# Scores of a product-key router by products with premultiplied weights: 512-column products on TensorE in place of 128-column queries and scores

## The reference, cut to what matters

```python
def peer(h, w_pq, sub_keys, u_tab, v_tab):
    B, N, D = h.shape                    # D = 1024
    T = B * N
    hf = h.reshape(T, D)
    q = (hf @ w_pq).reshape(T, PEER_HEADS, 2, PEER_HALF)          # 8 heads, 2 halves of 128
    s = jnp.einsum('thsd,hskd->thsk', q, sub_keys)                # 128 sub-keys per half
    s_top, i_top = lax.top_k(s, PEER_TOPK)                        # 16
    ...
```

## Time and profile before

| | us |
|---|---|
| median of 3 runs | 3248.2 (3245.08 to 3252.93) |
| profiled execution, its own time | 3257.12 |
| span of that profile | 3255.3 |
| PE busy | 3180.3 (98%) |
| DVE busy | 2619.6 (80%) |
| ACT busy | 1255.9 (39%) |
| POOL busy | 1592.9 (49%) |
| L1087 `query`, PE busy | 262.1 |

### The profile page before, as it was taken

One profiled execution on the slowest core, in us unless ns is written; L12 is line 12 of the kernel. 1 busy time (PEld: TensorE's weight loads), 2 busy tenths in 40 slices (PEclk: granted clock), 3 DMA queues, 4 the chain that ended last, 5 costly groups with the idle time before them and its releaser, 6 DMA issues.

```text
span 3255.3 us, 46922 instructions
## 1 busy us (share of the span) xinstructions
PE 3180.3 (98%) x17282; PEld 2784.5 (86%) x17282; DVE 2619.6 (80%) x5356; ACT 1255.9 (39%) x2309; POOL 1592.9 (49%) x999
## 2 busy tenths in 40 slices
PE   8999899999998899999999999999999999999998
PEld 5887588788877799898989999989999999999997
DVE  3333368888888799998989888889999998888876
ACT  3343334334426633333333333333433333333343
POOL 0300006788767388888888887323333332333310
PEclk9999999999999999999999999999999999999999
DMA  6924556676676799999999999989899999999963
GB/s 252 391 109 158 235 195 195 183 206 173 191 217 208 280 351 351 342 345 346 349 337 356 357 347 384 363 341 364 339 374 361 354 366 357 355 362 355 348 227 114
DMA packets 297746, 963.29 MB, mean 296 GB/s; under 512 B 94004, under 2 KB 148148, under 8 KB 238775
## 3 DMA queue, kind: packets, MB, share of 16 engines
q1 hardware_dynamic: 158680, 523.71, 43.9%
q0 software_dynamic: 138560, 436.55, 38.6%
q10 hardware_dynamic: 288, 0.16, 0.0%
HBM read 893.83 MB, written 66.49 MB: 295 GB/s over the span
## 4 chain that ended last, share of the span: by engine, by line
PE 47%; DVE 12%; DMA 5%; issue 1%; ACT 1%; SPq 0%; DVEq 0%; ACTq 0%
PE bank L1961 24%; PE bank L1971 23%; DMA work<-in_u 5%; DVE ring L2109 3%; DVE acc L2126 2%; DVE uL L2292 2%; DVE vL L2288 1%; DVE ga L2305 1%; DVE cL L2283 1%; ACT uR L2040 0%; ACT vR L2056 0%; DVE slots L2231 0%; DVE st L2258 0%; DVE work L2169 0%; DVE slots L2255 0%
## 5 line engine op out<-in xcount | busy, mean ns | idle before, releaser
L1923 POOL DMA_INDIRECT ring<-in_uv,slots x384 | 583.1, 1519 | 807.2 <-DVE carry L2126 698.1
L185 POOL DMA_INDIRECT g_cells<-slots x384 | 710.5, 1850 | 318.0 <-DVE slots L1639 199.7
L1961 PE MATMUL bank<-hR,uR 128*128 128x384 f32 x2032 | 684.9, 337 | 11.1 <-DVE uL L2292 11.0
L1961 PE MATMUL bank<-hR,uL 128*128 128x384 f32 x2032 | 684.3, 337 | 0.0
L1961 PE MATMUL bank<-hL,uR 128*128 128x384 f32 x2032 | 682.8, 336 | 0.0
L2048 ACT ACTIVATE cR<-ga 128x384 fp32r<-128x384 f32 x253 | 133.1, 526 | 945.2 <-PE bank L1971 569.1
L1971 PE MATMUL bank<-vR,cR 128*128 128x512 f32 x1518 | 472.8, 392 | 5.1 <-DVE cL L2283 4.5
L1971 PE MATMUL bank<-vR,cL 128*128 128x512 f32 x1518 | 471.1, 392 | 0.0
L1971 PE MATMUL bank<-vL,cR 128*128 128x512 f32 x1518 | 471.0, 391 | 0.0
L2109 DVE CUSTOM_DVE_ANT_0 ring<-ring,slots 128x1024 f32<-128x1024 f32 x384 | 467.2, 1254 | 1.9 <-DMA ring<-in_uv,slots 1.9
L1961 PEld LDWEIGHTS bank<-hR,uR 128*128 128x128 f32 x2032 | 383.2, 189 | 25.2 <-DVE uL L2292 15.6
(11 more groups left out here) (346 smaller groups left out, 4328.4 us busy)
## 6 DMA issues: line engine op xcount, KB each, us to landing
work<-in_v SPq DMA_DIRECT2D x256, 512.0 KB, 6.9
work<-in_u SPq DMA_DIRECT2D x254, 512.0 KB, 6.1
work<-in_w_pq SPq DMA_DIRECT2D x36, 2048.0 KB
work<-in_w_o SPq DMA_DIRECT2D x18, 2048.0 KB
g_cells<-work POOLq DMA_DIRECT2D x48, 512.0 KB, 5.6
work<-g_cells SPq DMA_DIRECT2D x32, 768.0 KB, 9.3
work<-g_blocks SPq DMA_DIRECT2D x31, 768.0 KB, 13.9
g_blocks<-big SPq DMA_DIRECT2D x8, 2048.0 KB, 6.8
```

The costliest lines, as they stand in the source:

```text
L185: pool.indirect_dma_start(out=cells_of(g_dram, i), out_offset=bass.IndirectOffsetOnAxis(ap=slots[:, i, D + k:D + k + 1].bitcast(U32), axis=0),
L1923: pool.indirect_dma_start(out=ring[:, k % R, :], out_offset=None, in_=a["uv"], in_offset=bass.IndirectOffsetOnAxis(ap=ids[:, k // P, k % P ...
L1961: mm = pe.matmul(A[t][:, 0:CW], w[t][:, k, :], h[:, k, :], start=(k == 0 and w is uR and h is hR), stop=(k == DK - 1 and w is uL))
```

## The change

In steps 3 to 6 PE multiplies the sub-keys into the query weights (`merge`): per step 8 banks of 4 products of 128 columns. ACT copies each bank into one of four buffers `merged` (it waits until the store four before has landed), and POOL stores each with a DMA of 256 KiB into a table `pq_scratch` in DRAM, 32 in all. From step 7 on, `score(i, g)` makes the scores at once by 8 products of 512 columns with the tile's rows held still and the stored table moving; `query`, its eviction and the buffer `qs` are gone. `sub` is loaded at the block's beginning instead of at step 4, and SP's order of 2 MiB loads has four new ones in it. DVE's two semaphores in `highest` become steps of its one chain semaphore, with the same waits.

```diff
+    MERGE = {3: 0, 4: 1, 5: 2, 6: 3}
...
+                    if key[0] == "score" and key[1] == 0:
+                        for m_out in merged_out:
+                            sp.wait_ge(m_out, FILLED + 2 * (key[2] + 1) * 16)
+                    part = key[1] if key[0] == "merge" else key[-1]
+                    src = {"mod": a["w_mod2"], "mix": a["w_o"], "merge": a["w_pqT"], "score": pq_dram}[key[0]]
+                    sp.dma_start(wr[:, at % 2, :], src[part, :, :]).then_inc(wr_in[at % 2], 16)
...
                         sp.wait_ge(w_mm, W["mod", 2] + 1)
+                        sp.dma_start(sub[:, :, :], a["sub"]).then_inc(const_in, 16)
                         load_x(0)
                         load_x(1)
+                        load("merge", 0, DK - 1)
...
+                    if n in MERGE and MERGE[n]:
+                        load("merge", MERGE[n], DK - 1)
                     if h == 1 and 0 <= i - 2 < NT:
-                        load("query", i - 2, 2)
+                        load("score", i - 2, 2)
...
+                for x in range(4 * DK):
+                    g, k = divmod(x, DK)
+                    pool.wait_ge(*emptied("merge", g, k))
+                    pool.dma_start(pq_dram[g, :, k * 512:(k + 1) * 512], merged[:, x % 4, :]).then_inc(merged_out[x % 4], 16)
...
-                def query(i, g):
+                def merge(g):
+                    if g == 0:
+                        pe.wait_ge(const_in, 16)
+                    w = weights("merge", g, DK - 1)
+                    for k in range(DK):
+                        ps = bank("merge", g, k)
+                        for l in range(4):
+                            mm = pe.matmul(ps[:, l * NKEY:(l + 1) * NKEY], w[:, l * D + k * P:l * D + (k + 1) * P],
+                                           sub[:, 4 * g + l, :], start=True, stop=True)
+                        mm.then_inc(w_mm, 1)
+
+                def score(i, g):
                     if g == 0:
                         pe.wait_ge(*emptied("turn", i, 0))
                         pe.wait_ge(*emptied("turn", i, 1))
-                    w, ps = weights("query", i, g), bank("query", i, g)
-                    for l in range(4):
-                        for k in range(DK):
-                            at = (l * DK + k) * P
-                            mm = pe.matmul(ps[:, l * P:(l + 1) * P], w[:, at:at + P], slots[:, i, k * P:(k + 1) * P],
-                                           start=(k == 0), stop=(k == DK - 1))
-                    mm.then_inc(w_mm, 1)
-
-                def score(i, g):
-                    ps = bank("score", i, g)
-                    pe.wait_ge(*emptied("query", i, g))
-                    if i == 0 and g == 0:
-                        pe.wait_ge(const_in, 48)
-                    for l in range(4):
-                        mm = pe.matmul(ps[:, l * NKEY:(l + 1) * NKEY], qs[:, g % 2, l, :], sub[:, 4 * g + l, :],
-                                       start=True, stop=True)
+                    w, ps = weights("score", i, g), bank("score", i, g)
+                    for k in range(DK):
+                        mm = pe.matmul(ps[:, :], slots[:, i, k * P:(k + 1) * P], w[:, k * 512:(k + 1) * 512],
+                                       start=(k == 0), stop=(k == DK - 1))
                     mm.then_inc(w_mm, 1)
...
-                def query(i, g):
-                    ps, f = bank("query", i, g)
-                    n = 4 * i + g
-                    if n >= 2:
-                        p = ("score", (n - 2) // 4, (n - 2) % 4)
-                        act.wait_ge(w_mm, W[p] + 1)
-                    act.activation(qs[:, g % 2, :, :], ps[:, :].rearrange("p (l t) -> p l t", l=4),
-                                   ACT.Copy).then_inc(f, 1)
+                def merge(g):
+                    for k in range(DK):
+                        ps, f = bank("merge", g, k)
+                        x = DK * g + k
+                        if x >= 4:
+                            act.wait_ge(merged_out[x % 4], FILLED + x // 4 * 16)
+                        act.activation(merged[:, x % 4, :], ps[:, :], ACT.Copy).then_inc(f, 1)
```

More of the change, by code:

```diff
@@ L64 @@
 EARLY = 16
+FILLED = (NZ // 4 + P // TB) * 16
 RATE = (2, 4)
@@ L248, in mixer_inputs @@
         junk = sq
-        zeroed = [sem(f"a_zero{k}") for k in range(4)]
+        pool_out = [sem(f"a_poolout{k}") for k in range(4)]
         zero_set, bias_in, pad_ready = sem("a_zset"), sem("a_bias"), sem("a_pad")
@@ L710, in _, with middle @@
                 finish(pe, NT - 1)
-def middle(nc, a, sb, sem, PS, ident, modc, sp1, silu, slots, carry, work, first_in, big, krT, kT, vv, front, mod_in, x1_dram, gate_dram, g_dram, placed, mix_dram, tile_in, tile_out, a_mm, a_ev, g_in, ga):
+    return pool_out
+def middle(nc, a, sb, sem, PS, ident, modc, sp1, silu, slots, carry, work, first_in, big, krT, kT, vv, front, mod_in, x1_dram, gate_dram, g_dram, placed, mix_dram, tile_in, tile_out, a_mm, a_ev, g_in, ga, pq_dram, merged_out):
     NH = NT * H
@@ L724, in number @@
         W[key] = len(W)
-        if key[0] in ("mix", "query") or key[0] == "mod" and key[1] in (3, 4):
+        if key[0] in ("mix", "score") or key[0] == "merge" and key[2] == DK - 1 or key[0] == "mod" and key[1] in (3, 4):
             WEIGHTS.append(key)
@@ L742, in middle @@
         if h == 1 and 0 <= i - 2 < NT:
-            number("query", i - 2, 2)
+            number("score", i - 2, 2)
         if h == 2:
-            if 0 <= i - 2 < NT and i - 1 != LAST:
-                number("score", i - 2, 2)
             if 0 <= i - 1 < NT:
@@ L762, in middle @@
             if 0 <= i - 1 < NT:
-                number("query", i - 1, 0)
-                number("query", i - 1, 1)
                 number("score", i - 1, 0)
+                number("score", i - 1, 1)
+        if n in MERGE:
+            for k in range(DK):
+                number("merge", MERGE[n], k)
     for ch_ in (6, 7):
@@ L1238, in _ @@
                         if 0 <= i - 1 < NT:
-                            query(i - 1, 0)
-                            query(i - 1, 1)
                             score(i - 1, 0)
+                            score(i - 1, 1)
+                    if n in MERGE:
+                        merge(MERGE[n])
                     if n == NH + 2:
@@ L1318, in spread @@
                         act.wait_ge(decoded, i)
+                    elif g == 0:
+                        for m_out in merged_out:
+                            act.wait_ge(m_out, FILLED + DK * 16)
                     sl = slice(4 * g, 4 * g + 4)
@@ L1418, in _ @@
                     if h == 2:
-                        if 0 <= i - 2 < NT and i - 1 != LAST:
-                            score(i - 2, 2)
                         if 0 <= i - 1 < NT:
@@ L1434, in _ @@
                             use(ch)
-                    if h == 0 and 0 <= i - 2 < NT:
-                        score(i - 2, 1)
                     if h == 0 and i - 1 == LAST:
@@ L1492, in highest @@
                         ins = dve.reduce_max(part[:, b:b + 1], PS[b][:, 0:width(n, b)], AX.X)
-                    ins.then_inc(m_part, 1)
-                    dve.wait_ge(m_part, n + 1)
-                    dve.reduce_max(mx[:, :], part[:, 0:groups(n)], AX.X).then_inc(m_max, 1)
-                    dve.wait_ge(m_max, n + 1)
+                    ch.step(ins)
+                    ch.step(dve.reduce_max(mx[:, :], part[:, 0:groups(n)], AX.X))
                     if n >= 2:
```

75 lines of the change are left out of this document (28 added, 47 removed).

## The result

The changed kernel takes 3265.94 us (median of 5 runs, 3263.57 to 3268.46), the kernel before 3249.65 in the same session (5 runs, 3245.08 to 3254.37). The ratio is 1.0044, 95% interval 1.0033 to 1.0055: slower by 0.44%. The forecast was 3246.2 with a range up to 3259, so the time lies outside it, on the slow side. A ratio is estimated from all the runs and can differ by about 0.1% from the quotient of two medians. The medians of the kernel before, run beside each group of experiments, lie from 3249.65 to 3252.43.

What follows compares the result with a forecast made beforehand. Attention block taken as bound by PE and an equally long DVE chain through norm; the merge's 29.3 us less savings of 31.3 gives -2.0 us, 3248.2 to 3246.2 us, with an 8-in-10 range of 3234 to 3259.

Steps and rivals of the forecast that it cites:

- the merge costs 29.3 us: Steps 3 to 6: the four merges, with their new waits, make step 7 begin 29.3 us later.
- the upper bound of 36: Steps 3 to 6: the most the four merges were to cost, 36 us; the lower bound was 24.4.
- 1 for stores: Step 3: 1 us added to the merge for its stores to DRAM.
- 1.5 for stores: Step 4: 1.5 us added to the merge for its stores to DRAM.
- The second weights: Step 4: the next merge weights, issued once mix's first half is used, take about 7 us for 2 MiB.
- The landing of the first weights: Step 3: the first merge's weights, with sub now ahead of them, land at 352.8.
- The tie of DVE's chain: Steps 12 to 31: DVE's run holds norm, so 2.7 us a tile arrive, 13.7 in all; 9.3 are given back.
- the rival that PE is the only bound: Steps 12 to 31: DVE's chain doesn't hold, the 9.3 us arrive too, 3232 to 3237; chance 0.17.
- The last attention head ends in step 35 and with it this tie: From step 32 to DVE's third one_hot unit: eight groups save 9.3 us; 11.5 us taken for the stretch.
- the 7.5 of the text: Block's tail: the part of the saving that falls behind the last mix, some 7.5 us.
- POOL was not hidden: Block's end: POOL's scatters end at 1073, the load needing the last at 1077, so just hidden.
- the merge's transfers stall PE: Steps 3 to 5: ACT waits for stores, PE for weights; at 5 us more per merge 3266; chance 0.15.

Runs made afterwards that it cites:

- holding the loads back: Changed kernel, four buffers; SP holds two 2 MiB loads (first half of mix, merge(2)) until a merge's first four stores have landed: 3261.86 us, ratio 1.0031.
- decode first: Changed kernel with DVE's decode ahead of the maxima at h = 0 (tiles 3 to 8), ACT's spread ahead of turned: 3247.94 us, ratio 0.9997.
- The twin kernel: Kernel before with only the 8 MiB DRAM table declared and never used: 3250.73 us, ratio 1.0001.
- the shortened DVE operation: Changed kernel with one operation of residual_in cut from 1024 to 8 columns: 3254.46 us, ratio 1.0015.
- both repairs: Changed kernel with eight merged buffers in place of four, and DVE's decode ahead of the maxima at h = 0: 3242.47 us, ratio 0.9971.

## Why the prediction was wrong, point by point

**The step that failed is the merge's price**, "so the merge costs 29.3 us": it cost 39.5, over the upper bound of 36 too. Two of its terms were mis-sized and one was missing.
- *Stores.* I gave "1 for stores" in step 3 and "1.5 for stores" in step 4, and had written in the bounds that in a full queue a store is "2 to 4 us late in each of steps 3 and 4". The lateness in the bounds came true: PE stood 2.99 and 4.06 us. I took the idle landing of the earlier trace rows as the value and left the loaded one for the range. Eight buffers, which remove just this, gave back 7.7 us, 5.9 of them beyond scatter; holding the loads back gave back 8.5.
- *The clock after a stand.* I counted a start at 1.2 GHz in step 3 only, as 2.7 us for which I showed no row. That size was about right: the eight banks of step 3 took 9.13 us without the stand, 2.0 over 7.15, and 9.13, 9.46 and 10.06 in the three kernels with eight buffers. For steps 4 and 5 I had put it at nothing. In step 5 the first attention products and the banks behind the stand ran partly at the low clock: six banks took 7.15 us instead of 5.36, the attention 7.35 instead of 6.1. Together 3.0 us, where step 5 was over by 2.9. In step 4 the two banks behind the stand took 3.58 us instead of 1.79, at a granted clock of 0.50. With eight buffers step 4 had no stand, and the attention of step 5 took 6.1 again (400.87 - 394.77), but the banks behind `high` 8.34.
- *The second weights* were reckoned to land 7 us after their issue; from 382.71 (369.74 + 6.1 + 6.87) to 391.16 it was 8.45. With 2.6 for the stand and 1.8 for the clock this makes 5.8 of the 6.2 us that step 4 was over.

The landing of the first weights (352.8 predicted, 357.62 less the 5.0 us of the late first block is 352.6) and step 6 (16.6, measured 16.62) held.

**The tie of DVE's chain held.** "Two chains of equal length lie side by side, and the change shortens one": 15.6 us arrived in the five tiles where PE alone would have given 23 (9.3 more than the 13.7 forecast), PE waited for `norm` at both places named, by 0.4 to 0.8 us, and shortening DVE by 1.06 us shortened the tile by 1.00. Only its size was off: 3.1 us a tile arrived instead of 2.7. With it the rival that PE is the only bound (3232 to 3237) is refuted in the changed kernel, and made true in the kernel with decode first, 67.17 us a tile against the 67.2 that I had given for it.

**"The last attention head ends in step 35 and with it this tie"** was half right. Step 32 still has its `decode`, and steps 32 to 35 took 70.35 us where decode first makes them 66.56. Of the 11.5 us forecast from step 32 on, 9.4 came: 2.0 up to step 36 and 7.4 behind it, against the 7.5 of the text.

**POOL was not hidden, though this cost nothing that shows.** The prediction had the scatters end at 1073, 4 us before the load that needs the last of them. They ended at 1115.67 - 21.19 = 1094.5, or 1089.5 without the 5.0 us of the late first block: 16.5 later than reckoned. Some 10 of these are the merge, the rest the scatters themselves, which took 482.1 us from 612.35 on where the kernel before took 475.5 from 577.27. The load then waited for them, as SP's waits of 1040 to 1160 us show:

```profile
SPq L958 <- DMA g_blocks<-slots: 6.5, 1, 6.5
```

The kernel before has no such wait. The load went out at 1098.66, 17.0 us before the block's end instead of 23.2. The experts lost nothing by it: they took 2.0 us less than before.

**From the trace to the median.** I let the changed kernel's profile stand 8.9 us over its runs, as that of before did. It stood 2.5 over. Of the 19.7 us between forecast and result, 10.3 are the block (10.2 of it the merge), 6.4 this assumption, and 3.0 the first block and the experts. The twin kernel points to what was behind most of the 6.4: with the same work its block was 5.6 us shorter than that of the profiled execution of before, by 3.2 in the very steps from 1 to 7 on which the merge's price was reckoned and by 2.3 behind step 36. Against the two undisturbed traces of the kernel before (63.8 and 63.9 us from step 1 to step 7) the merge costs 42.6, as much as the ratios give for leaving it out.

**The rival that came true, in part,** is "the merge's transfers stall PE". Each merge had to lose over 2.1 us more than I gave it, and on average they lost 2.6 (10.2 / 4): 1.1 up to step 4, 6.2 in step 4, 2.9 in step 5 and none in step 6. In step 5 no transfer was waited for, so the transfers and the clock behind their stands account for 7.3, or 1.8 a merge. That the time is close to the 3266 written there is chance, since 9.5 of its 19.7 us over the forecast are no part of the merge. I gave it 0.15, because the DMA share in steps 4 to 6 would be lower than at 340 to 360 us. It was (0.72, 0.74 and 0.54 over the three windows of 20 us from 360 to 420), and the mean hid the case that counts, a 2 MiB load issued just as the stores begin.

## What to carry to other kernels

- Where a buffer's turn fits with nothing to spare in an idle queue, take the landing beside the loads that the program issues at that moment, not the idle one. Here the difference was some 6 to 8 us, and four more buffers removed it.
- Before taking work from the engine that is busy for 100% of a stretch, look for the engine that hands it its next input, and shorten both chains: here a reorder on DVE, worth less than nothing before, was worth 12 us after the change.
- One trace of before is one execution. Where the sum rests on a stretch of 30 us, a second trace of the same code tells how much of it is scatter (3 us here; in the changed kernel's merges 4, from 102.3 to 106.6 us in the four kernels in which neither buffers nor loads differ).

## What was not expected of the hardware

The same stand was followed by a different clock from one kernel to the next. In step 5 PE stands 2.87 us behind two full banks in six of these kernels, and then does the same six banks. Its timeline in the kernel with decode first and four buffers:

```profile
410.89 5.74 PE L1096 MATMUL bank<-front,work 128*128 128x128 f32 x48 [2.87 <-ACT front L1306]
416.47 0.27 PE L1141 MATMUL bank<-ident,on 128*128 128x128 f32 x1
```

There the banks took 5.58 us at a granted clock of 1.00. They took 6.93 at 0.79 with the shortened DVE operation, 7.15 at 0.76 in the changed kernel, 7.15 with the stores by ACT, 7.17 with both repairs, and 8.34 at 0.64 with eight buffers. These are single executions, and what decides among them stays open.

In step 35 the low clock fell ahead of a wait in one kernel and behind it in others. The timeline of PE in the changed kernel, and the row in the kernel with the loads held that stands before its stand of 2.95 us (shown above):

```profile
922.44 3.80 PE L1158 MATMUL bank<-big,prT 128*128 128x128 f32 x18
...
928.43 13.97 PE L1106 MATMUL bank<-work,slots 128*128 128x512 f32 x32 [1.32 <-ACT slots L1298]
```

```profile
912.70 2.17 PE L1164 MATMUL bank<-big,prT 128*128 128x128 f32 x18
```

In the changed kernel the granted clock was 0.79 from 920 to 928 us: the products of `values` took 3.80 us, PE waited only 1.32 for the eviction, and the two groups behind it took 13.97 at a clock of 1.00. With the loads held the same products took 2.17, the wait was 2.95, and the groups took 16.88, at 0.82 from 918 to 936 us. With the shortened DVE operation it was 2.96 and 16.98, at 0.83 from 916 to 935. From the start of those products to the next step the three took 19.8, 22.7 and 22.8 us. So the 3 us are not the price of 1.6 us more of waiting: in the first kernel the low clock fell on short work ahead of the wait, in the two others on the groups. Why it fell there stays open too.
